# First FFN weight units of a macaron diffusion layer started inside the conditioning stage, and the context scaled on VectorE

## What is computed

```python
mx = split(silu(c) @ ada_w + ada_b, 9)        # for the latent tokens
mc = split(silu(c_ctx) @ ada_w + ada_b, 9)    # for the context tokens
x = x + 0.5 * mx[2] * swiglu(modulate(rmsnorm(x, g1), mx[0], mx[1]), w1, w3, w2)
y = y + 0.5 * mc[2] * swiglu(modulate(rmsnorm(y, g1), mc[0], mc[1]), w1, w3, w2)
hc = modulate(rmsnorm(y, g_mix), mc[3], mc[4])
pc = hc @ w_in[:, :3072]                      # keys of two directions, values
s_f, s_b = final states of the two recurrences over pc
px = modulate(rmsnorm(x, g_mix), mx[3], mx[4]) @ w_in
x = x + mx[5] * (concat(hgrn(px, s_f, s_b), hyena(px, filters)) @ w_out)
x = x + 0.5 * mx[8] * swiglu(modulate(rmsnorm(x, g2), mx[6], mx[7]), w1b, w3b, w2b)
out = rmsnorm(x, g_final)
```

## Time and profile before

| | us |
|---|---|
| median of 3 runs (3038.76 to 3040.71) | 3040.64 |
| the profiled execution | 3041.57 |
| its span in the trace | 3039.7 |
| first FFN matmul | 129.95 |
| first context matmul | 1581.04 |
| TensorE busy | 2971.9 (98%) |
| VectorE busy | 2059.7 (68%) |
| ScalarE busy | 1164.0 (38%) |
| GpSimd busy | 180.5 (6%) |
| DMA read from HBM | 551 MB, mean 183 GB/s |

### The profile page before, as it was taken

One profiled execution on the slowest core, in us unless ns is written; L12 is line 12 of the kernel. 1 busy time (PEld: TensorE's weight loads), 2 busy tenths in 40 slices (PEclk: granted clock), 3 DMA queues, 4 the chain that ended last, 5 costly groups with the idle time before them and its releaser, 6 DMA issues. The chain is left out here.

```text
span 3039.7 us, 42630 instructions
## 1 busy us (share of the span) xinstructions
PE 2971.9 (98%) x15878; PEld 2529.7 (83%) x15878; DVE 2059.7 (68%) x2656; ACT 1164.0 (38%) x1479; POOL 180.5 (6%) x213
## 2 busy tenths in 40 slices
PE   6899999999999999999989999999999999999998
PEld 2488888888888888888879999999998888888886
DVE  4678776676767667674477767778866666666657
ACT  3322222222222222222247777754345444444444
POOL 1000000000000000000040033330000000000001
PEclk9999999999999999999999999999999999999999
DMA  9866455454566758573335555446565666666664
GB/s 354 318 210 192 146 159 181 143 186 132 164 202 222 249 178 277 191 249 96 97 78 166 171 164 153 153 146 183 165 194 167 191 189 192 189 189 189 192 190 150
DMA packets 369792, 559.07 MB, mean 184 GB/s; under 512 B 18111, under 2 KB 260152, under 8 KB 368776
## 3 DMA queue, kind: packets, MB, share of 16 engines
q1 hardware_dynamic: 364112, 544.62, 57.2%
q0 software_dynamic: 2640, 8.52, 0.8%
q10 hardware_dynamic: 2920, 4.29, 0.4%
HBM read 551.06 MB, written 6.30 MB: 183 GB/s over the span
## 5 line engine op out<-in xcount | busy, mean ns | idle before, releaser
L421 DVE TENSOR_TENSOR w_lo<-raw,w_hi 128x1024 fp32r<-128x1024 f32 x736 | 913.1, 1242 | 675.5 <-ACT w_hi L416 673.7
L416 ACT ACTIVATE w_hi<-raw 128x1024 fp32r<-128x1024 f32 x736 | 777.3, 1059 | 1479.2 <-PE bank L433 1095.1
L431 PE MATMUL bank<-h_hi,w_hi 128*128 128x512 f32 x1472 | 573.9, 390 | 3.0 <-issue 3.0
L433 PE MATMUL bank<-h_hi,w_lo 128*128 128x512 f32 x1472 | 573.4, 390 | 0.0
L432 PE MATMUL bank<-h_lo,w_hi 128*128 128x512 f32 x1472 | 573.3, 389 | 0.0
L653 DVE SCALAR_TENSOR_TENSOR states<-ada_raw,silu_c,states 128x1024 f32<-128x1024 f32 x300 | 375.7, 1280 | 2.3
L431 PEld LDWEIGHTS bank<-h_hi,w_hi 128*128 128x128 f32 x1472 | 276.7, 188 | 62.7 <-issue 5.1
L432 PEld LDWEIGHTS bank<-h_lo,w_hi 128*128 128x128 f32 x1472 | 276.6, 188 | 57.6 <-issue 0.2
L433 PEld LDWEIGHTS bank<-h_hi,w_lo 128*128 128x128 f32 x1472 | 276.7, 188 | 57.5
L431 PE MATMUL bank<-hx_hi,w_hi 128*128 128x256 f32 x1024 | 295.2, 288 | 0.0
L433 PE MATMUL bank<-hx_hi,w_lo 128*128 128x256 f32 x1024 | 289.6, 283 | 0.0
(11 more groups left out here) (323 smaller groups left out, 4029.1 us busy)
## 6 DMA issues: line engine op xcount, KB each, us to landing
raw<-in_ffn_w_dram SPq DMA_DIRECT2D x528, 512.0 KB, 4.2
ada_raw<-in_ada_w_dram SPq DMA_DIRECT2D x256, 512.0 KB, 4.6
raw<-in_w_in_dram SPq DMA_DIRECT2D x176, 512.0 KB, 3.7
raw<-in_ada_w_dram SPq DMA_DIRECT2D x32, 512.0 KB, 10.4
raw<-in_w_out_dram SPq DMA_DIRECT2D x32, 512.0 KB, 3.7
spec_spill<-spec_out ACTq DMA_DIRECT2D x4, 1024.0 KB, 13.6
spec<-spec_spill POOLq DMA_DIRECT2D x8, 512.0 KB, 3.9
xin<-in_x_dram SPq DMA_DIRECT2D x1, 2048.0 KB, 9.5
```

Source lines behind the costliest of these rows:

```text
L416: nc.scalar.activation(w_hi[un.slot(j)][:], raw[un.slot(j)][:], ACT.Copy).then_inc(hi_done, 1)
L421: nc.vector.tensor_tensor(w_lo[un.slot(j)][:], raw[un.slot(j)][:], w_hi[un.slot(j)][:].bitcast(F32), ALU.subtract).then_inc(lo_done, 1)
L431: nc.tensor.matmul(o, w_hi[slot][:, c0:c0 + P], hi, start=start, stop=False, skip_group_check=True)
L433: return nc.tensor.matmul(o, w_lo[slot][:, c0:c0 + P], hi, start=False, stop=stop, skip_group_check=True)
```

## The change

- Sixteen landing places for the conditioning units instead of eight: the eight tiles of `w_hi` and `w_lo` are used too (`ada_ahead`), for units 0 to 31; units 32 to 39 use eight of them, units 40 to 63 the four of `ada_raw`. Their uses have their own semaphore, `cond_used`.
- The first stage ends after 48 steps (`TAIL`). Conditioning units 48 to 63 run within the first four FFN weight units, in pairs after the first and the third of a unit's four blocks (`inside`). The third and fourth sums are turned into columns within weight units 1 and 4.
- The order of the first 16 weight units: six units that need only feature blocks 0 to 7 come first, two of them for the other half of the columns, in banks 4 and 5. The first six are loaded among the conditioning loads (`FIRST_LOADS_AT`).
- Feature blocks 0 to 7 of the FFN input are all made in steps 35 to 43, beside the filters, blocks 8 to 15 in weight units 4 to 6. Conditioning of the fifth sum (`HALF_AT`) moves from weight units 2 to 15 to 6 to 15.
- Filter quarters start at steps 10, 18, 28, 36 (before 12, 22, 32, 42). The product for the taps goes in halves, each when its banks are free; the spill goes in two DMAs of 0.5 MB from two tiles, and both must have landed before either half of the next quarter is evicted.
- `xin` and `yin` no longer share memory with the taps; `ang` moves into `root` and `rstd`.
- Context: GpSimd's two passes go; VectorE scales (`ctx_scaled`), two blocks ahead. In the first round the first eight units alternate between part 0 and part 1 of the same `kg`; its gates come at unit 7, logarithms at 8, running sums at 8 to 11, the first decay at 10, the latent blocks at 7 to 10.

The diff, cut to its core:

```diff
-WIDE = 8
-PLAIN = range(ADA_UNITS)
+
+A_AT, R_AT, H_AT, L_AT = 0, 4, 8, 12
+LAND = list(range(16)) * 2 + [A_AT, A_AT + 1, A_AT + 2, A_AT + 3, H_AT + 2, H_AT + 3, L_AT + 2, L_AT + 3] + [A_AT, A_AT + 1, A_AT + 2, A_AT + 3] * 6
...
-SPEC_FIRST, SPEC_EVERY = 12, 10
+SPEC_AT = (10, 18, 28, 36)
...
+        ahead = ExitStack()
+        ada_ahead = [sb(f"ada_ahead{s}", [P, UNIT], scope=ahead) for s in range(2 * RING)]
+        ahead.close()
...
+            def up(un, j, kg, part, sub, c, each=None, inside=None):
+
+                first = isinstance(c, int) and c == 0
+                if kg == 0 and not (first and (sub == 0 or part == 0)):
+                    pe.wait_ge(s["gmul" if part else "silu"], c * FBLK + (2 * sub))
+                b0 = 4 if first and sub and not part else 2 * part
+                col_unit(pe, un, j, kg, [out(b0), out(b0 + 1)], hi, lo, False, each, inside)
...
+                if inside and k < 3:
+                    inside(j, k)
             last.then_inc(w_used, 1)
+            if inside:
+                inside(j, 3)
...
-        FIRST_UP = [(0, part, kg) for kg in range(4) for part in range(2)] + [(1, part, kg) for part in range(2) for kg in range(4)]
+        FIRST_UP = ([(0, part, kg) for kg in range(2) for part in range(2)] + [(1, 0, 0), (1, 0, 1)]
+                    + [(0, part, kg) for kg in range(2, 4) for part in range(2)] + [(1, 0, 2), (1, 0, 3)] + [(1, 1, kg) for kg in range(4)])
+        UP_LOADED = 6
...
+        FIRST_LOADS_AT = (39, 41, 45, 50, 56, 62)
...
+            if landed_before(g):
+                sy.wait_ge(cond_used, landed_before(g)[-1] + 1)
+            sy.dma_start(ada_wide[LAND[g]][:], ada_w[m * P:(m + 1) * P, half * HALF:(half + 1) * HALF]
+                         ).then_inc(wide_sem(g), 16)
...
+        CTX_PLACE = [[(j // 4, j % 4) for j in range(12)] for _ in range(PAIRS)]
+        CTX_PLACE[0][0:8] = [(part, kg) for kg in range(4) for part in range(2)]
+        LATENT_MOD_AT = [(7, 8, 9, 10)] + [(4, 6, 8, 10)] * (PAIRS - 1)
...
+                if g in FIRST_LOADS_AT:
+                    load_first(sy, FIRST_LOADS_AT.index(g))
...
-            for kb in range(KB):
-                po.wait_ge(fa["bfree"], KB * N_CHUNK + kb + 1)
-                nc.gpsimd.tensor_scalar(zc[:, kb, :], y_res[:, kb, :], scale_a[:, 1, kb, 1:2], None, ALU.mult).then_inc(nctx["zc"], 1)
-            po.wait_ge(nctx["rstd"], 1)
-            for kb in range(KB):
-                po.wait_ge(nctx["zc"], kb + 1)
-                if kb >= 4:
-                    po.wait_ge(nctx["lo"], kb - 3)
-                nc.gpsimd.tensor_tensor(xn_at(1, kb, 0), zc[:, kb, :], rstd[:, SEQ:2 * SEQ], ALU.mult).then_inc(nctx["xn"], 1)
...
-        SQUARES_AT, SUM_AT, ROOT_AT, DIAG_AT, NORM_AT, SPREAD_AT = (5, 5, 7, 7, 11, 11, 12, 12), 20, 21, 22, 28, 29
-        ROW_AT, TURN_AT, TAKE_AT = (17, 33, 49), (18, 36, 52), (19, 37, 53)
-        L1_AT, INVERSE_AT = (22, 32, 42, 54), (23, 33, 43, 55)
-        MOD_FIRST, MOD_EARLY = 56, 5
+        SQUARES_AT, SUM_AT, ROOT_AT, DIAG_AT, NORM_AT, SPREAD_AT = (5, 5, 7, 7, 11, 11, 12, 12), 14, 14, 15, 24, 25
+        ROW_AT, TURN_AT, TAKE_AT = (17, 33), (18, 34), (19, 34)
+        TURN_TO = (4, 4, 4, 6)
+        TAIL = 48
+        L1_AT, INVERSE_AT = (20, 28, 38, 46), (21, 29, 39, 47)
+        MOD_FIRST = 35
+        FIRST_ROUND_AT = (41, 43, 45)
...
+            def inside(j, k):
+                g = TAIL + 4 * j + k
+                if k in (0, 2) and g < ADA_UNITS:
+                    unit(g)
+                    unit(g + 1)
+                if (j, k) == (1, 1):
+                    to_columns(2)
+                if (j, k) == (3, 3):
+                    pe.wait_ge(cols_done, 4)
+                    pe.wait_ge(ada_out, 4)
+                if (j, k) == (4, 1):
+                    to_columns(3)
...
+                    part, kg = CTX_PLACE[it][j]
+                    col_unit(pe, un, j, kg, [bank[part][:, 0:256], bank[part][:, 256:512]],
+                             lambda k: hc_hi[:, k, :], lambda k: hc_lo[:, k, :], True, nctx["lo"] if it == 0 and part == 0 else None)
...
-                if q and o == 0:
-                    ac.wait_ge(fs_dma, 16 * q)
+                if q:
+                    ac.wait_ge(fs_dma, 32 * q)
                 ac.wait_ge(fs_spec, 2 * q + o + 1)
-                nc.scalar.activation(spec_out[:, 2 * o, :], bank[2 * o][:], ACT.Copy).then_inc(fs_even, 1)
-
-            def spill(q):
-                ac.wait_ge(fs_out, 4 * q + 4)
-                dst = spec_dram[q // 2][:, :, q % 2 * 512:(q % 2 + 1) * 512]
-                ac.dma_start(dst, spec_out[:]).then_inc(fs_dma, 16)
-
-            for o in range(ADA_UNITS):
+                nc.scalar.activation(spec_out[o][:, 0, :], bank[2 * o][:], ACT.Copy).then_inc(fs_even, 1)
+
+            def spill(q, o):
+                ac.wait_ge(fs_out, 4 * q + 2 * o + 2)
+                dst = spec_dram[q // 2][:, 2 * o:2 * o + 2, q % 2 * 512:(q % 2 + 1) * 512]
+                ac.dma_start(dst, spec_out[o][:]).then_inc(fs_dma, 16)
+
+            for o in range(TAIL):
...
-                if 0 <= o - MOD_FIRST - 2 < MOD_EARLY + 1:
-                    if o == MOD_FIRST + 2:
-                        ac.wait_ge(fs_spec, 8)
-                    modulate_act(ac, n1, 0, n1["hi_ap"], (0, 1), o - MOD_FIRST - 2, o - MOD_FIRST - 1)
-            round_unit(ac, Units(U_FFN1), 0)
-            modulate_act(ac, n1, 0, n1["hi_ap"], (0, 1), 6, 7)
-            row_out(ADA_BEFORE - 1)
-            round_unit(ac, Units(U_FFN1), 1)
-            modulate_act(ac, n1, 0, n1["hi_ap"], (0, 1), 7, 8)
-            round_unit(ac, Units(U_FFN1), 2)
+                    if (q := spec_step(o, 8 + 2 * n)) is not None:
+                        spill(q, n)
+                if 0 <= o - MOD_FIRST - 1 < 8:
+                    modulate_act(ac, n1, 0, n1["hi_ap"], (0, 1), o - MOD_FIRST - 1, o - MOD_FIRST)
+                if o in FIRST_ROUND_AT:
+                    round_unit(ac, Units(U_FFN1), FIRST_ROUND_AT.index(o))
+            row_out(2)
...
             def early_hi(j):
-                if j < 4:
-                    modulate_act(ac, n1, 0, n1["hi_ap"], (0, 1), 8 + 2 * j, 10 + 2 * j)
+                if j == 3:
+                    row_out(3)
+                    ac.wait_ge(fs_dma, 32 * 4)
+                if 4 <= j < 7:
+                    modulate_act(ac, n1, 0, n1["hi_ap"], (0, 1), (8, 12, 14)[j - 4], (12, 14, 16)[j - 4])
...
-            low1(5)
-            rest_unit(ve, Units(U_FFN1), 0)
-            scaled1(7)
-            low1(6)
-            rest_unit(ve, Units(U_FFN1), 1)
-            ve.wait_ge(fs_dma, 16 * 4)
-            low1(7)
-            rest_unit(ve, Units(U_FFN1), 2)
-            take(ADA_BEFORE - 1)
-            ve.wait_ge(mod_done, 6)
-            scaled1(8)
-            scaled1(9)
+                if 0 <= o - MOD_FIRST - 1 < 8:
+                    low1(o - MOD_FIRST - 1)
+                    if o - MOD_FIRST + 1 < 8:
+                        scaled1(o - MOD_FIRST + 1)
+                if o in FIRST_ROUND_AT:
+                    rest_unit(ve, Units(U_FFN1), FIRST_ROUND_AT.index(o))
...
             def early_lo(j):
-                for kb in range(8 + 2 * j, min(10 + 2 * j, KB)):
-                    low1(kb)
-                    if kb + 2 < KB:
-                        scaled1(kb + 2)
+                if j == 1:
+                    take(2)
+                if j == 4:
+                    take(3)
+                    ve.wait_ge(mod_done, 6)
+                    ve.wait_ge(fs_dma, 32 * 4)
+                    scaled1(8)
+                    scaled1(9)
+                if 4 <= j < 7:
+                    for kb in range((8, 12, 14)[j - 4], (12, 14, 16)[j - 4]):
+                        low1(kb)
+                        if kb + 2 < KB:
+                            scaled1(kb + 2)
...
+            def ctx_scaled(kb):
+                scaled(ve, nctx, 1, [y_res], (1,), kb, SEQ)
+
             rstd_dve(ve, nctx, (1,))
-            ctx_low(0, 8)
+            ve.wait_ge(nctx["rstd"], 1)
+            ctx_scaled(0)
+            ctx_scaled(1)
+            for kb in range(6):
+                ctx_low(kb, kb + 1)
+                ctx_scaled(kb + 2)
```

More of the change, by code:

```diff
@@ L66, with landed_before, last_in @@
 ADA_UNITS = ADA_BEFORE * KB
-WIDE = 8
-PLAIN = range(ADA_UNITS)
+A_AT, R_AT, H_AT, L_AT = 0, 4, 8, 12
+LAND = list(range(16)) * 2 + [A_AT, A_AT + 1, A_AT + 2, A_AT + 3, H_AT + 2, H_AT + 3, L_AT + 2, L_AT + 3] + [A_AT, A_AT + 1, A_AT + 2, A_AT + 3] * 6
+def landed_before(g):
+    return [e for e in range(g) if LAND[e] == LAND[g]]
+def last_in(place):
+    return max(g for g in range(ADA_UNITS) if LAND[g] == place)
 HALF_ORDER = (0, 2, 1, 3)
@@ L208, in build @@
         hid = [sb(f"hid{n}", [P, SEQ], scope=first) for n in range(3)]
-        ang = [sb(f"ang{n}", [P, SEQ], scope=first) for n in range(4)]
+        ang = [half[:, n * SEQ:(n + 1) * SEQ] for half in (root, rstd) for n in range(2)]
```

(32 more changed lines are left out.)

220 lines of the change are left out of this document (105 added, 115 removed).

## The result

The changed kernel takes 3045.36 us (median of 17 runs, 3044.04 to 3048.28) beside 3040.37 for the kernel before on the same chip: a ratio of 1.0018, 95% interval 1.001 to 1.0025. It is 5 us slower, where I had forecast 12.5 us faster. The profiled execution took 3044.45 us.

What follows compares the result with a forecast made beforehand. TensorE was taken as the bound, busy for 98% of 3039.7 us, with DMA nearly full in the first stage; 3041.57 - 7.6 (part A) - 5.0 (Part B) - 0.9 (to the median) gave 3028.1 us, range 3020 to 3040.

Steps and rivals of the forecast that it cites:

- part A: First stage: FFN starts at 112.6 us with 9.75 us of moved work behind it; gains 7.6 us, between 1 and 13.
- rival 2: FFN start: VectorE's list later or longer, transfers late; 7 us lost, 3035; chance 0.25 together with Rival 4.
- three signs that I had named for a wrong forecast: ScalarE waiting several us for `spec_spill`; TensorE for `ada_raw` in the FFN; waits for `h1_lo` in weight units 6 to 9.
- my list: VectorE's operations from 78.0 us to the FFN start, summing to 34.2 us without rest.
- Part B: Context: TensorE starts 2.9 us earlier and later waits of 2.1 us go; gains 5.0 us, between 1 and 8.
- Rival 1: FFN: each of sixteen changes between full-width matmuls and 32-column units costs 0.2 us, 3.2 us together, 3031.3; chance 0.14.
- Rival 3: First stage: evictions wait for both spill halves; 13 us at a 13.6 us landing, 3047 from 17 us; chance 0.09.
- Rival 4: First stage: moved work not covered, zero gain there, only Part B left: 3035.6; chance 0.25 together with rival 2.

Runs made afterwards that it cites:

- experiment 1: Changed kernel with the fifth sum's half-unit loads issued two weight units further back in SyncE's queue: 3032.0 us, ratio 0.9975.
- experiment 2: Kernel before with only the new `HALF_AT` step table: 3052.39 us, ratio 1.004; with the loads also two weight units further back: 3040.2 us, ratio 1.0.
- experiment 4: Kernel of experiment 1 with the context as in the kernel before: 3037.59 us, ratio 0.9992.
- experiment 5: Kernel of experiment 1 with bounds and lane masks moved into the first FFN weight unit: 3030.06 us; also feature blocks 4 to 7 made last: 3025.94 us.
- experiment 3: Kernel before with only the change's context part: 3033.17 us, ratio 0.9979; with only the context scaling moved to VectorE, old order: 3036.09 us, ratio 0.9989.
- experiment 6: Kernel of experiment 1 with the sixteen moved conditioning units in four groups of four instead of eight pairs: 3034.5 us, ratio 0.998.

## Why the prediction was wrong

**The step that failed** is one sentence of part A: that the conditioning steps moved to weight units 6 to 15 leave VectorE "a backlog of 3 us against weight remainders prepared three units ahead. Nothing." The work was sized rightly (two steps 4.87 us and a remainder 1.14, 6.0 us a unit where I had 6.1), and experiments 1 and 2 show that by itself it costs nothing. What I left out was the other end of the same steps: each is also a DMA issue in SyncE's in-order queue that waits for a step four earlier, with the next weight load behind it. For the conditioning loads of the first 64 units I did ask what a load waits for; for those of the fifth sum, which the diff moves only through a table, I asked only about VectorE. The cost is 12.7 us alone (experiment 2), and 12.7 in the changed kernel (1). None of my rivals held it: rival 2's late transfers were for the first weight units. Of the three signs that I had named for a wrong forecast, two occurred, both small: TensorE waited for `ada_raw` inside the FFN (0.39 and 0.54 us before the second units of two pairs), and ScalarE for a spill (2.6 us, below). The wait for `w_lo` stood in no list.

**Part A otherwise.** Forecast 7.6 us; with the queue mended it gives 2.6 (experiment 4, whose interval just reaches no change), 3.5 by the landmark in the changed kernel. TensorE's idle time ahead of the FFN, which this part was to win, fell only from 24.0 to 21.2 us. The start: forecast 112.6, measured 114.41. VectorE ended `tdif` of the third quarter at 79.9 rather than 78.0, which is the difference. VectorE, against the earlier trace rows:

```profile
78.76 1.22 DVE L2114 TENSOR_TENSOR tdif<-taps 128x1024 f32<-128x1024 f32 x1
...
84.64 0.48 DVE L517 SCALAR_TENSOR_TENSOR xn<-x_res,scale_a,rstd 128x256 f32<-128x256 f32 x1
...
107.78 1.22 DVE L434 TENSOR_TENSOR w_lo<-raw,w_hi 128x1024 fp32r<-128x1024 f32 x1
```

From 79.9 to 114.4 are 34.5 us, where my list had 34.2 and 0.4 of hand-overs. The sum was right to 0.1 us, though not its terms: VectorE worked for 32.65 us and was idle for 1.85. It was the engine that decided, as experiment 5 shows. TensorE, busy for 79% of the stage as before, was granted a clock of 0.85 in it (0.93 before). What that cost is not shown; it may be why `tdif` came late, since in 60 to 70 us, where TensorE was busy without a gap at a granted 0.83, four conditioning units took it 3.32 us, and in the kernel of experiment 1, at 1.00, they took 1.92 (where the wait for the spill, below, made `tdif` late instead). The loss at the FFN start (0.70 in 114.4 to 120) is about what it was before (0.66 in 130 to 135). Behind the start, the first four weight units took 35.6 us where I had 31.5 (four times 5.44, 8.8 and 0.95), or 33.2 with the clock loss that before had there too. Of the 2.3 us over, 0.7 are pairs at 1.19 for 1.1, 0.9 the waits for `ada_raw`; 0.7 I can't assign. So A's mechanism held and its size was 4 us too large, 1.8 of it at the start and 2.3 behind it.

**Part B** was forecast at 5.0 us, and gave 6.1 between the end of the FFN and the last context matmul in the changed kernel, 6.2 in experiment 3, and 6.6 by its medians. The start of the context, against the earlier trace rows (TensorE, then VectorE; GpSimd has no row there any more):

```profile
1588.69 0.36 PE L444 MATMUL bank<-hc_hi,w_hi 128*128 128x256 f32 x1 [2.64 <-DVE hc_lo L528]
...
1585.21 1.75 DVE L501 RECIPROCAL rstd<-root 128x256 f32<-128x256 f32 x1 [1.96 <-ACT root L1779]
1588.05 0.49 DVE L528 SCALAR_TENSOR_TENSOR hc_lo<-xn,mods,hc_hi 128x256 fp32r<-128x256 f32 x1 [0.18 <-ACT hc_hi L548]
```

From the first sum-of-squares matmul to the first context matmul are 6.39 us, before 9.22: 2.8 earlier, forecast 2.9. A low part takes 0.48 us where it took 0.93 beside GpSimd. The two later waits (2.2 us) are gone, as forecast. The clock falls as before, only a little later (0.66 in 1590 to 1595). Of the remaining 1.1 us, waits for `w_lo` in the context could be 0.4 (1.3 us for 1.7 before); but the kernel of experiment 1 has 2.3 us of them and takes no longer for this stretch. I leave them open. The stretch behind the context was taken as unchanged; it is 1.5 us shorter in the changed kernel. That doesn't come from the change: in the eleven traces this stretch takes either 1302.9 or 1304.3 us, and two kernels with the old first stage (steps moved only, scaling alone) have the shorter value too.

**The rivals.** Rival 1, the switch, was real and nearly of its size: 0.17 us for each of sixteen changes, 2.6 us, though 1.8 of it lay hidden in my 1.1 for a pair that costs 0.88 when it stands behind another. Rival 2, a later start and late transfers, came in small: 1.8 us at the start and 0.9 us of waits, where it had 7. Rival 3, the spill on the path, did not come: ScalarE waited for a spill once, for 2.6 us, where the second half, issued at 59.23, had landed by 69.13, less than 10 us, and TensorE ran on without a gap meanwhile. It was close: in the kernel of experiment 1 the same wait was 4.4 us, and TensorE stood for 1.47 us behind it. Rival 4, no gain at all from part A, would have given 3035.6, nearer to the result than my 3028.1. The mended kernel, which is what I had thought that I was pricing, takes 3032.0, half-way between the two.

**The range.** Its upper end, 3040, was made of costs of the parts that I had priced. An unpriced queue was outside it by construction. Of the chance of 0.08 for slower, 0.06 was put on the spill and 0.02 on rivals 2 and 4, none on this. By my own bounds the 3045.36 still falls into the 0.20 for no change that can be told (under 3046.7); the interval, 1.001 to 1.0025, shows that it is slower all the same.

## What to carry to other kernels

When work is moved, follow both of its ends: what the engine has to do at the new place, and when the transfer that feeds it is issued, what that issue waits for, and what stands behind it in the same in-order queue. If the awaited step itself stands behind data that this queue has just loaded, the whole round trip (here 13 us: landing, rounding, remainder, two steps) bounds the loop, and it shows in the profile as a stretch in which every engine is idle. Moving an issue behind two more loads cost nothing and brought 13 us, more than both intended parts together.

## What the runs showed of the hardware

- A change between 128 x 128 and 128 x 32 tiles and back costs TensorE 0.33 us between running matmuls (experiment 6).
- After 7.06 us of idling TensorE ran at 0.63 us a matmul, the 1.2 GHz level, for 5.3 us; after 2.17 us of idling soon behind it, it ran on at full clock. So one wait of 7 us cost about 2.9 us more than its length.
- A low part of 128x256 took VectorE 0.93 us beside GpSimd's multiplications and 0.48 us without them (part B).
- A first stage of the same code ended at times 3.5 us apart in four kernels, with granted clocks of 0.62, 0.73, 0.77 and 0.98 in 100 to 110 us. Which comes from which is open; 3.0 us of it are there before 81 us. The first stage of the kernel before, in five traces, ended from 128.53 to 130.80. A gain ahead of the FFN of one or two microseconds can't be read from one trace.
